# A mixture-of-experts loop: tokens gathered in four pieces and turned by VectorE, the down product copied by ScalarE alone

## The chip, the core and the metric

The kernel runs on one core of a Trainium2 chip. The metric is the device time of one execution in microseconds (us); the median of three runs before the change is 2490.03 us (2484.62 to 2492.65).

## What is computed

One decoder layer for 2048 tokens of width 1024: a mixer (windowed attention beside a gated recurrence), layer norm, and a mixture of experts: one shared expert and 64 routed ones, 8 for each token. The part that this change is about, from the reference, cut:

```python
def _moe(h, w_router, e_bias, w_gate, w_up, w_down, ws_gate, ws_up, ws_down):
    ...
    # pairs (token, expert) sorted by expert, padded to blocks of MOE_BLOCK = 128
    def body(acc, blk):
        toks, bw, e = blk
        xb = hp[toks]
        yb = (jax.nn.silu(xb @ w_gate[e]) * (xb @ w_up[e])) @ w_down[e]
        return acc.at[toks].add(yb.astype(f32) * bw[:, None]), None
```

All data is float32. Each product is made as three: every operand is split into a high part, rounded for TensorE (type `fp32r`), and the low rest, and high x high, high x low and low x high are summed.

## The kernel before

The program runs in phases: `mixer`, `output_and_route` (which leaves the table `htab`, one row of 1024 values and 64 expert weights for each token), `place_and_share` (which works out the token list of every block, `idx`, and half of the shared expert), `experts`, and `share_and_norm`. `experts` is a loop over blocks of 128 tokens, two blocks to a turn; an expert has as many blocks as its tokens fill. Its order is written out by hand: each engine has its own instruction stream (`block.tensor`, `block.vector`, `block.scalar`, `block.gpsimd`, `block.sync`) and they meet at semaphores.

For one block, in step n of the loop:

- GpSimd gathers the rows of block n+4 from `htab` into `xg` (128 tokens x 1088 values, `gather`, line 2301; its indices are first copied to `gi` by line 2298), copies the indices of block n to `si` (line 2319), and adds `y` to the rows of `acc` in DRAM by an indirect DMA (the scatter, line 2326). The scatter waits until the scatter before it has landed (`added`), since two blocks can hold one token.
- TensorE does the low part of gate and up for block n+1 (`gate_up_low`, line 2514, 8 matmuls), the down product of block n into `psY`, two halves of 512 columns (line 2559, 12 matmuls), the high part of gate and up for block n+2 (`gate_up_high`, line 2503, 16 matmuls), the turn of `H` (line 2521, 2 transposes into `psH`), and the turn of the tokens of block n+3 (`turn_x`, line 2487, 8 transposes of 128 x 128 into `psX`).
- ScalarE makes the high parts: `HT_hi`, `xT_hi` (line 2340, twice 512 columns out of `psX`), the silu into `sg`, the first half of `y` (line 2395), and, where a new expert begins, the high parts of the next expert's weights (line 2344: two pieces of gate and up, one of down).
- VectorE makes the low parts: `HT_lo` (line 2466), `xT_lo` (line 2406, twice), `pairw` (each token's weight for the expert, line 2434), `H` (line 2443), the second half of `y` (line 2476), and the low parts of the next weights (line 2409, three times 2048 columns for an expert).
- SyncE loads the raw weights of later experts (line 2284), two slots ahead, once `gulo_s` and `dlo_s` say that a slot's low parts are made.

`carry_wait` is a semaphore increment behind a wait; it costs an issue slot and nothing else.

## Time and profile before

| | us |
|---|---|
| median of three runs | 2490.03 |
| the profiled execution's own time | 2485.66 |
| its span in the profile | 2483.8 |
| `experts` loop, about | 853 to 2390 |
| TensorE busy | 2382.5 (96%) |
| VectorE busy | 1575.5 (63%) |
| ScalarE busy | 1161.9 (47%) |
| GpSimd busy | 767.3 (31%) |

A group of the profile gives a source line, the engine, the operation, destination and sources by the program's tile names, how often it ran, its busy time and mean duration, and the time that the engine was idle just before, with what ended most of that idle time. A timeline lists instructions by their start. Waits, semaphores and register instructions are not counted as busy. For DMAs, packets are counted by queue: queue 0 carries what GpSimd issues (gathers and scatters), queue 1 what SyncE issues (weights, in the loop); the share is of all 16 DMA engines' time.

### The profile page before, as it was taken

What the parts mean: (1) busy time and instruction counts of PE and PEld (TensorE: products, weight loads), DVE (VectorE), ACT (ScalarE), POOL (GpSimd) and SP (SyncE); (2) the same over time, 40 slices, a digit from 0 to 9 for tenths busy, and PEclk for the clock granted to TensorE, in tenths of its full rate; (3) what the DMA queues carried; (4) which work ended last, traced back from release to release, by engine and by line L of the source; (5) the groups of instructions that cost most, each with busy time, mean ns of one, the idle gap of its engine ahead of it and who ended that gap; (6) DMA issues with size and microseconds to landing.
All of it is one profiled execution on the core that took longest, in us unless ns stands there. A gap on an engine that the chain in (4) does not pass through costs nothing. (4 is left out here: it accounts for less than half of the span.)

```text
span 2483.8 us, 49979 instructions
## 1 busy us (share of the span) xinstructions
PE 2382.5 (96%) x11840; PEld 1954.7 (79%) x11842; DVE 1575.5 (63%) x2285; ACT 1161.9 (47%) x1621; POOL 767.3 (31%) x829
## 2 busy tenths in 40 slices
PE   8899999989997799999999999999999999999986
PEld 6677777678886688888888888888888888888875
DVE  6686867768878756555665555656665556655447
ACT  4525253542225645445554445545554445544334
POOL 0010100011110134334543433534443334444327
PEclk9999999989998899999999999999999999999998
DMA  7242323364445579778988878888888789987863
GB/s 254 77 144 98 111 94 111 117 218 164 171 164 206 196 230 284 223 219 270 273 259 233 254 218 263 268 266 262 257 253 243 224 223 274 283 247 222 216 221 136
DMA packets 253808, 524.34 MB, mean 211 GB/s; under 512 B 18065, under 2 KB 165169, under 8 KB 249649
## 3 DMA queue, kind: packets, MB, share of 16 engines
q1 hardware_dynamic: 204464, 336.64, 39.7%
q0 software_dynamic: 48672, 186.86, 29.4%
q8 instruction: 36, 0.59, 0.1%
q14 instruction: 28, 0.22, 0.0%
q10 hardware_dynamic: 608, 0.02, 0.0%
HBM read 386.61 MB, written 136.87 MB: 211 GB/s over the span
## 5 line engine op out<-in xcount | busy, mean ns | idle before, releaser
L2503 PE MATMUL psG<-gu_split,xT_hi 128*128 x2624 | 624.3, 390 | 2.9 <-ACT xT_hi L2340 1.5
L2503 PEld LDWEIGHTS psG<-gu_split,xT_hi 128*128 128x128 f32 x2624 | 493.8, 188 | 106.2 <-issue 3.6
L2326 POOL DMA_INDIRECT acc<-y,si x162 | 290.1, 1791 | 728.6 <-DMA acc<-y,si 413.3
L2409 DVE TENSOR_TENSOR gu_split<-raw_gu,gu_split (+1 forms) x127 | 290.6, 2288 | 175.3 <-ACT gu_split L2344 171.7
L2514 PE MATMUL psG<-gu_split,xT_lo 128*128 x1304 | 339.3, 402 | 5.9 <-issue 5.8
L2514 PEld LDWEIGHTS psG<-gu_split,xT_lo 128*128 128x128 f32 x1304 | 233.1, 188 | 50.1 <-issue 8.7
L2344 ACT ACTIVATE gu_split<-raw_gu x126 | 234.3, 1907 | 33.5 <-issue 33.5
L2301 POOL DMA_INDIRECT xg<-htab,gi x164 | 205.0, 1250 | 130.4 <-POOL gi L2298 109.7
L2409 DVE TENSOR_TENSOR d_lo<-raw_d,d_hi (+1 forms) x64 | 146.7, 2292 | 149.5 <-ACT d_hi L2344 149.5
L2389 ACT ACTIVATE HT_hi<-psH 128x256 fp32r<-128x256 f32 x162 | 62.4, 385 | 351.6 <-PE psH L2521 351.6
L2406 DVE TENSOR_TENSOR xT_lo<-psX,xT_hi 128x512 fp32r<-128x512 f32 x328 | 209.7, 680 | 8.5 <-ACT xT_hi L2340 8.5
L2476 DVE COPY y<-psY 128x512 f32<-128x512 f32 x162 | 111.4, 688 | 154.0 <-PE psY L2559 154.0
L2559 PE MATMUL psY<-d_hi,HT_hi 128*128 x648 | 199.9, 390 | 0.0
L2559 PE MATMUL psY<-d_lo,HT_hi 128*128 x648 | 199.7, 389 | 0.0
L2559 PE MATMUL psY<-d_hi,HT_lo 128*128 x648 | 199.6, 389 | 0.0
L2340 ACT ACTIVATE xT_hi<-psX 128x512 fp32r<-128x512 f32 x328 | 178.5, 596 | 17.6 <-PE psX L2487 9.2
L2487 PE MATMUL psX<-ident,xg 128*128 128x128 f32 x1320 | 171.7, 273 | 4.2 <-PEq L1639 4.2
L2376 ACT ACTIVATE sg<-psG 128x256 f32<-128x256 f32 x163 | 62.6, 384 | 204.3 <-PE psG L2514 204.3
L2344 ACT ACTIVATE d_hi<-raw_d (+1 forms) x64 | 122.7, 1917 | 74.6 <-PE psY L2559 74.5
L2487 PEld LDWEIGHTS psX<-ident,xg 128*128 128x128 f32 x1320 | 149.3, 141 | 4.7 <-issue 4.6
L2466 DVE TENSOR_TENSOR HT_lo<-psH,HT_hi 128x256 fp32r<-128x256 f32 x162 | 67.8, 418 | 131.0 <-ACT HT_hi L2389 130.5
L2395 ACT ACTIVATE y<-psY 128x512 f32<-128x512 f32 x162 | 95.6, 590 | 102.5 <-PE psY L2559 98.4
(388 smaller groups left out, 3723.7 us busy)
## 6 DMA issues: line engine op xcount, KB each, us to landing
raw_gu<-in_w_gate_dram SPq DMA_DIRECT2D x64, 1024.0 KB, 6.0
raw_gu<-in_w_up_dram SPq DMA_DIRECT2D x64, 1024.0 KB
raw_d<-in_w_down_dram SPq DMA_DIRECT2D x64, 1024.0 KB, 6.9
wring<-split_d SPq DMA_DIRECT2D x24, 1024.0 KB, 4.8
split_d<-wring POOLq DMA_DIRECT2D x8, 1024.0 KB, 4.2
raw_d<-mixed SPq DMA_DIRECT2D x16, 512.0 KB, 3.9
xt<-in_x_dram SPq DMA_DIRECT2D x16, 512.0 KB, 4.3
htab<-h SPq DMA_DIRECT2D x16, 512.0 KB, 2.6
```

The costliest lines, as they stand in the source:

```text
L2301: nc.gpsimd.indirect_dma_start(out=xg[slot][:], out_offset=None, in_=htab, in_offset=bass.IndirectOffsetOnAxis(ap=gi[slot][:, 0:1], axis=0 ...
L2326: nc.gpsimd.indirect_dma_start(out=acc, out_offset=bass.IndirectOffsetOnAxis(ap=si[k][:, 0:1], axis=0), in_=y[k][:], in_offset=None, compu ...
L2340: nc.scalar.activation(xT_hi[slot][:, h * HALF:(h + 1) * HALF, :], psX[h][:], ACT.Copy).then_inc(xhi_s[h], 1)
L2344: nc.scalar.activation(dst, src, ACT.Copy).then_inc(done, 1)
L2395: nc.scalar.activation(y[k][:, 0:512], psY[:, 0, :], ACT.Copy).then_inc(y_s[0], 1)
L2406: nc.vector.tensor_tensor(xT_lo[slot][:, at, :], psX[h][:], xT_hi[slot][:, at, :], ALU.subtract).then_inc(xlo_s[h], 1)
L2409: nc.vector.tensor_tensor(dst, src, hi, ALU.subtract).then_inc(dlo_s if n == 2 else gulo_s, 1)
L2476: nc.vector.tensor_copy(y[k][:, 512:], psY[:, 1, :]).then_inc(y_s[1], 1)
L2487: m = nc.tensor.transpose(psX[half][:, c, :], xg[slot][:, (half * HALF + c) * P:(half * HALF + c + 1) * P], ident[:])
L2503: nc.tensor.matmul(psG[slot][:], xT_hi[slot][:, c, :], right[:, bass.ds(w, 1), c, :].rearrange("p a n -> p (a n)"), start=(n == 0 and c == ...
L2514: m = nc.tensor.matmul(psG[slot][:], xT_lo[slot][:, c, :], gu_hi[:, bass.ds(w, 1), c, :].rearrange("p a n -> p (a n)"), start=False, stop= ...
L2559: m = nc.tensor.matmul(psY[:, h, :], left[:, c, :], right[:, bass.ds(w, 1), c, h * 512:(h + 1) * 512].rearrange("p a n -> p (a n)"), start ...
```

## The change

The table `htab` now has each row in four pieces (`QUADS`): 256 values and the weights of 16 experts, 272 values in all (`PIECE`). A gather is four indirect DMAs (`gather_pieces`, new line 1636), each with 128 indices. The indices are made ahead for all blocks (`pidx`), so that the piece g of partition group a holds quarter a of the tokens 32g to 32g+31. VectorE's transpose, which turns squares of 32 x 32, then gives the complete turn of the block: `xF`. To fit, value d of a token lies at chunk d mod 8 of partition d div 8, and the gate and up weights are loaded by rows in the same order (`by_run`, "(p k) n -> p k n"). The weights of the pairs are turned with them and turned back by one TensorE transpose into `psW`, from where `pairw` is read. `xT_hi` and `xT_lo` are made out of `xF` in SBUF, each by one instruction of 1024 columns. The whole of `y` is one ScalarE copy, and ScalarE also writes `gi` and `si`.

The core of the diff:

```diff
+def gather_pieces(nc, htab, to, at, done):
+    for g in range(QUADS):
+        nc.gpsimd.indirect_dma_start(out=to[:, g, 0:PIECE], out_offset=None, in_=htab.rearrange("r a w -> (r a) w"),
+                                     in_offset=bass.IndirectOffsetOnAxis(ap=at[:, g:g + 1], axis=0)).then_inc(done, 16)
...
@@ place_and_share, GpSimd @@
-            pool.wait_ge(idx_s, 2)
             for k in range(2):
-                nc.gpsimd.tensor_copy(gi[k][:], idx[:, k:k + 1]).then_inc(gi_s, 1)
+                nc.gpsimd.memset(xg[k][:, :, PIECE:WIDE], 0.0).then_inc(tails_s, 1)
+            pool.wait_ge(idx_s, 3)
...
@@ place_and_share, VectorE @@
+                for a in range(QUADS):
+                    for g in range(QUADS):
+                        last = nc.vector.tensor_scalar(pidx[a * QP:(a + 1) * QP, :, g], idx[g * QP:(g + 1) * QP, :], float(QUADS), float(a),
+                                                       ALU.mult, ALU.add)
...
@@ experts, GpSimd, in the loop @@
-                    pool.wait_ge(turned[1], s.n + 3)
-                    pool.wait_ge(pairw_s, s.n + 3)
+                    pool.wait_ge(next_gi_s, s.n + 1)
                     carry_wait(pool, passed)
-                    gather(s.n + AHEAD, k, s.n + AHEAD + 1)
-                    nc.gpsimd.tensor_copy(si[k][:], idx[:, bass.ds(s.n, 1)]).then_inc(si_s, 1)
+                    gather_pieces(nc, htab, xg[k], gi[k], x_in[k])
                     s.wait(pool, si_s)
-                    for h in range(2):
-                        s.wait(pool, y_s[h])
+                    s.wait(pool, y_s)
...
@@ experts, ScalarE @@
+            def high_x(nth, slot):
+                act.wait_ge(turned_s, nth)
+                nc.scalar.activation(xT_hi[slot][:], xF[slot][:, 0:KC, :], ACT.Copy).then_inc(xhi_s, 1)
...
-                    evac_x(s.n + 3, k)
+                    high_x(s.n + 3, k)
+                    gather_index(s.n + AHEAD, k)
...
-                    s.wait(act, yps_s[0])
-                    act.wait_ge(added[k], s.turn * 16)
-                    nc.scalar.activation(y[k][:, 0:512], psY[:, 0, :], ACT.Copy).then_inc(y_s[0], 1)
+                    s.wait(act, yps_s[1])
+                    scatter_index(s, k)
+                    nc.scalar.activation(y[k][:], psY[:].rearrange("p a b -> p (a b)"), ACT.Copy).then_inc(y_s, 1)
...
@@ experts, VectorE @@
+            def turn_x(slot, gathered, ahead):
+                dve.wait_ge(x_in[slot], gathered * 16 * QUADS)
+                if ahead is not None:
+                    dve.wait_ge(wturn_s, ahead)
+                    dve.wait_ge(xhi_s, ahead)
+                nc.vector.transpose(xF[slot][:, 0:KC, :].rearrange("p c (g j) -> p c g j", g=QUADS),
+                                    xg[slot][:, :, 0:D // QUADS].rearrange("p g (i c) -> p c g i", c=KC))
+                nc.vector.transpose(xF[slot][:, KC, :].rearrange("p (g j) -> p g j", g=QUADS),
+                                    xg[slot][:, :, D // QUADS:WIDE]).then_inc(turned_s, 1)
...
-                    for h in range(2):
-                        evac_x(h, s.n + 3, k)
                     s.wait(dve, H_s)
-                    pair_weight(nexts[n + 1], k, s.turn + 2)
+                    pair_weight(nexts[n], s.n + 2, 1 - k)
+                    low_x(s.n + 3, k)
                     product(s.n + 2, 1 - k)
+                    turn_x(1 - k, s.turn + k + 2, s.n + 2)
                     when_first(dve, nexts[n + 1], lambda: split(nexts[n + 1], 0))
-                    s.wait(dve, yps_s[1])
-                    dve.wait_ge(added[k], s.turn * 16)
-                    nc.vector.tensor_copy(y[k][:, 512:], psY[:, 1, :]).then_inc(y_s[1], 1)
                     when_first(dve, nexts[n + 1], lambda: split(nexts[n + 1], 1))
...
@@ experts, TensorE, at the end of a step @@
-                    pe.wait_ge(x_in[1 - k], (s.turn + k + 2) * 16 )
-                    for h in range(2):
-                        pe.wait_ge(xlo_s[h], s.n + 3)
-                        turn_x(1 - k, h)
+                    turn_weights(s.n + 3, k)
...
@@ weight loads, gate and up alone @@
-                        sp.dma_start(dst, w[0, bass.ds(e, 1)].rearrange("a (k p) n -> p (a k) n", p=P)).then_inc(sm, 16)
+                        rows = "a (k p) n -> p (a k) n" if sm is down_in else "a (p k) n -> p (a k) n"
+                        sp.dma_start(dst, w[0, bass.ds(e, 1)].rearrange(rows, p=P)).then_inc(sm, 16)
```

The stores and loads of `htab` rows in the phases before the loop follow the new layout; the 64 weights of a token go out as four runs of 16, one DMA for a tile of tokens where one for two tiles stood.

What stands on VectorE from `HT_lo` to the first weight split of a step, before (names as in the list above; ISA and REGISTER_ALU rows are waits and address arithmetic):

```order
L2466 TENSOR_TENSOR HT_lo<-psH,HT_hi 128x256
L2404 REGISTER_ALU
L2406 TENSOR_TENSOR xT_lo<-psX_0,xT_hi 128x512
L2406 TENSOR_TENSOR xT_lo<-psX_1,xT_hi 128x512
L2432 ISA
L2434 REGISTER_ALU
L2434 ISA
L2434 COPY pairw<-xg 128x1
L2438 REGISTER_ALU
L2443 SCALAR_TENSOR_TENSOR H_1<-psG_1,pairw,sg 128x256
```

And after the change:

```order
L2505 TENSOR_TENSOR HT_lo<-psH,HT_hi 128x256
L2468 REGISTER_ALU
L2470 REGISTER_ALU x2
L2470 ISA
L2470 COPY pairw<-psW 128x1
L2441 REGISTER_ALU
L2442 TENSOR_TENSOR xT_lo<-xF,xT_hi 128x1024
L2479 SCALAR_TENSOR_TENSOR H_1<-psG_1,pairw,sg 128x256
L2430 ISA
L2435 STREAM_TRANSPOSE xF<-xg 128x1024
L2437 STREAM_TRANSPOSE xF<-xg 128x128
```

The two `xT_lo` out of PSUM have become one out of `xF`, behind `pairw` now, and the turn of the next block's tokens (`STREAM_TRANSPOSE`, two instructions) follows `H`.

On GpSimd one block of the loop, before, from the index copy `gi` of the gather to the scatter:

```order
L2298 COPY gi<-idx 128x1
L2299 REGISTER_ALU
L2301 DMA xg<-htab,gi 128x1088
L2319 ISA
L2319 COPY si<-idx 128x1
L1099 REGISTER_ALU
L2324 REGISTER_ALU
L2326 DMA acc<-y_0,si 2176x1024
```

And after the change:

```order
L2335 ISA
L1636 DMA xg<-htab,gi 128x272 x4
L2340 REGISTER_ALU
L2342 DMA acc<-y_0,si 2176x1024
```

Both index copies have left GpSimd, and four DMAs of 128 x 272 stand where one of 128 x 1088 stood.

On VectorE just ahead of the loop, in `place_and_share`, where the block lists `idx` become ready, before and after:

```order
L1945 TENSOR_SCALAR some<-psRank 128x192
L1946 TENSOR_TENSOR idx<-none,some 128x192
L1947 TENSOR_SCALAR idx<-zr,blockno 128x4
L2030 TENSOR_TENSOR gu_split<-raw_gu,gu_split 128x2048
```

```order
L1958 TENSOR_SCALAR some<-psRank 128x192
L1959 TENSOR_TENSOR idx<-none,some 128x192
L1960 TENSOR_SCALAR idx<-zr,blockno 128x4
L1965 TENSOR_SCALAR pidx<-idx 32x196 x16
L2049 TENSOR_TENSOR gu_split<-raw_gu,gu_split 128x2048
```

Sixteen instructions for `pidx` stand between `idx` and the split of the first expert's weights.

## Rows read from the trace of the kernel before

**Rows 1.** The page: its span.

```profile
span 2483.8 us, 49979 instructions
```

**Rows 2.** Windows: us, busy of each engine, clock, DMA share, GB/s.

```profile
1500.00:2000.00 500.00, 496.82 (x2455) 416.43 (x2454) 291.43 (x384) 251.57 (x331) 206.31 (x216) 1.00 0.86 252
```

**Rows 3.** Timeline of TensorE, one block: start us, us, line, operation, count.

```profile
1513.30 0.38 PE L2521 MATMUL psH<-ident,H 128*128 128x128 f32 x2
1513.52 1.04 PE L2487 MATMUL psX<-ident,xg 128*128 128x128 f32 x8
1514.31 2.09 PE L2514 MATMUL psG<-gu_split,xT_lo 128*128 x8
...
1518.95 3.79 PE L2503 MATMUL psG<-gu_split,xT_hi 128*128 x16
1522.59 0.38 PE L2521 MATMUL psH<-ident,H 128*128 128x128 f32 x2
```

**Rows 4.** Tile psH over the loop: ns min/median/max, first and last start.

```profile
L2521 PE MATMUL psH<-ident,H x322: 270/271/272, 880.1 to 2373.8; 128*128 128x128 f32 x161
```

**Rows 5.** Groups on VectorE in the loop: busy us, mean ns, idle before.

```profile
L2409 DVE TENSOR_TENSOR gu_split<-raw_gu,gu_split x124 | 283.7, 2288 | 171.7 <-ACT gu_split L2344 171.7
L2406 DVE TENSOR_TENSOR xT_lo<-psX,xT_hi 128x512 fp32r<-128x512 f32 x322 | 205.9, 680 | 8.3 <-ACT xT_hi L2340 8.3
L2409 DVE TENSOR_TENSOR d_lo<-raw_d,d_hi x62 | 142.1, 2292 | 148.9 <-ACT d_hi L2344 148.9
L2476 DVE COPY y<-psY 128x512 f32<-128x512 f32 x161 | 110.7, 688 | 152.0 <-PE psY L2559 152.0
L2443 DVE SCALAR_TENSOR_TENSOR H<-psG,pairw,sg 128x256 f32<-128x256 f32 x161 | 77.1, 479 | 32.0 <-ACT sg L2376 31.9
L2466 DVE TENSOR_TENSOR HT_lo<-psH,HT_hi 128x256 fp32r<-128x256 f32 x161 | 67.3, 418 | 130.5 <-ACT HT_hi L2389 130.5
```

**Rows 6.** A group on ScalarE in the loop, same columns.

```profile
L2340 ACT ACTIVATE xT_hi<-psX 128x512 fp32r<-128x512 f32 x322 | 175.1, 596 | 8.3
```

**Rows 7.** The scatter on GpSimd in the loop, same columns.

```profile
L2326 POOL DMA_INDIRECT acc<-y,si x161 | 288.5, 1792 | 726.3 <-DMA acc<-y,si 413.3 <-DVE pairw L2434 146.3 <-DVE y L2476 56.8
```

**Rows 8.** Gather and scatter on GpSimd: ns min/median/max, first and last start.

```profile
L2301 POOL DMA_INDIRECT xg<-htab,gi x161: 1004/1007/3114, 884.1 to 2377.7; - x161
L2326 POOL DMA_INDIRECT acc<-y,si x162: 1583/1607/2717, 878.4 to 2381.2; - x162
```

**Rows 9.** Timeline of VectorE and GpSimd, start and us: a wait for the port.

```profile
1300.11 2.28 DVE L2409 TENSOR_TENSOR gu_split<-raw_gu,gu_split  x1
...
1301.18 2.69 POOL L2326 DMA_INDIRECT acc<-y,si  x1 [3.99 <-DVE y L2476]
```

**Rows 10.** DMA queues, 1200 to 1600 us: packets, MB, share of 16 engines.

```profile
q0 software_dynamic: 12121, 45.52, 45.0%
q1 hardware_dynamic: 41648, 55.17, 41.3%
```

**Rows 11.** Line 2326, the scatter: time to landing.

```profile
DMA to landing us min/median/max: 6.0/7.5/11.4
```

**Rows 12.** DMA queue 0, 2382 to 2389 us: one scatter alone.

```profile
q0 software_dynamic: 144, 0.52, 48.8%
```

**Rows 13.** DMA queue 0, 2372.5 to 2382 us: one scatter, one gather.

```profile
q0 software_dynamic: 288, 1.08, 53.7%
```

**Rows 14.** Timeline of SyncE: issues of gate weights for three experts.

```profile
1330.62 0.38 SPq L2284 DMA_DIRECT2D raw_gu<-in_w_gate_dram  x1
...
1358.48 0.38 SPq L2284 DMA_DIRECT2D raw_gu<-in_w_gate_dram  x1
...
1377.05 0.38 SPq L2284 DMA_DIRECT2D raw_gu<-in_w_gate_dram  x1
```

**Rows 15.** Timeline of VectorE before the loop starts.

```profile
839.59 0.36 DVE L1945 TENSOR_SCALAR some<-psRank 128x192 f32<-128x192 f32 x1
...
852.94 2.29 DVE L2409 TENSOR_TENSOR gu_split<-raw_gu,gu_split 128x2048 fp32r<-128x2048 f32 x1 [3.06 <-PEq L1639]
```

More of the change, by code:

```diff
@@ L2128, in _, with load_expert, experts @@
                     down(n)
-def load_expert(eng, w_gate, w_up, w_down, expert, slot, wgu, wd, loaded):
+def load_expert(eng, w_gate, w_up, w_down, expert, slot, wgu, wd, loaded, by_run=False):
     for w, sm, dst in zip((w_gate, w_up, w_down), loaded, (wgu[:, slot, :, 0:FE], wgu[:, slot, :, FE:], wd[:, slot])):
-        eng.dma_start(dst, w[0, expert].rearrange("(k p) n -> p k n", p=P)).then_inc(sm, 16)
-def experts(nc, passed, w_gate, w_up, w_down, ident, htab, acc, table, n_turns, idx, xg, gi, gi_s, x_in, acc_out, gu, guhi_s, gulo_s, wgu, wd, loaded, y, si, added,
+        rows = "(p k) n -> p k n" if by_run and w is not w_down else "(k p) n -> p k n"
+        eng.dma_start(dst, w[0, expert].rearrange(rows, p=P)).then_inc(sm, 16)
+def experts(nc, passed, w_gate, w_up, w_down, ident, htab, acc, table, n_turns, idx, pidx, tails_s, xg, gi, gi_s, x_in, acc_out, gu, guhi_s, gulo_s, wgu, wd, loaded, y, si, added,
             prefetch_shared, prefetch_hT):
@@ L2166, in experts @@
         psG = [ps(f"psG5_{i}", [P, 2 * FE]) for i in range(2)]
-        psX = [ps(f"psX5_{i}", [P, HALF, P]) for i in range(2)]
+        psW = ps("psW5", [P, P])
         psH = ps("psH5", [P, 512])
@@ L2203, in __init__, with column @@
                 self.word = word
-            def expert(self):
-                return within(self.word & (EXPERTS - 1), 0, EXPERTS - 1)
+            def column(self):
+                share = EXPERTS // QUADS
+                return within((self.word & (EXPERTS - 1)) + (self.word & (EXPERTS - share)), 0, P - 1)
             def next(self):
@@ L2483, in _, with turn_weights @@
         def _(pe):
-            def turn_x(slot, half):
-                for c in range(HALF):
-                    m = nc.tensor.transpose(psX[half][:, c, :], xg[slot][:, (half * HALF + c) * P:(half * HALF + c + 1) * P], ident[:])
-                m.then_inc(turned[half], 1)
+            def turn_weights(nth, slot):
+                pe.wait_ge(turned_s, nth)
+                if not (isinstance(nth, int) and nth == 1):
+                    pe.wait_ge(pairw_s, nth - 1)
+                carry_wait(pe, passed)
+                nc.tensor.transpose(psW[:], xF[slot][:, KC, :], ident[:]).then_inc(wturn_s, 1)
             def gate_up_high(nth, slot, entry):
-                for h in range(2):
-                    pe.wait_ge(xhi_s[h], nth)
+                pe.wait_ge(xhi_s, nth)
                 pe.wait_ge(gulo_s, entry.rank() * 2)
@@ L2535, in _ @@
             turn_H(0)
-            pe.wait_ge(x_in[0], 32)
-            for h in range(2):
-                pe.wait_ge(xlo_s[h], 2)
-                turn_x(0, h)
+            turn_weights(2, 1)
             def body(i):
@@ L2545, in body @@
                     gate_up_low(s.n + 2, 1 - k, words[n + 1])
-                    for h in range(2):
-                        s.wait(pe, y_s[h], behind=1)
+                    s.wait(pe, y_s, behind=1)
                     pe.wait_ge(dlo_s, r)
@@ L3122, in decoder_layer @@
         si = [sb(f"si{i}", [P, 1], I32) for i in range(2)]
-        experts(nc, passed, w_gate, w_up, w_down, ident, htab, acc, table, n_turns, idx, xg, gi, gi_s, x_in, acc_out, gu, guhi_s, gulo_s, raw_gu, raw_d,
+        experts(nc, passed, w_gate, w_up, w_down, ident, htab, acc, table, n_turns, idx, pidx, tails_s, xg, gi, gi_s, x_in, acc_out, gu, guhi_s, gulo_s, raw_gu, raw_d,
                 loaded, y, si, added,
```

134 lines of the change are left out of this document (71 added, 63 removed).

## Prediction

> **What bounds the kernel now.** I read the page first, for the span [rows 1], then the windows, then single steps. In the window from 1500 to 2000 us TensorE is busy 496.8 of 500 us at granted clock 1.00, and the DMA engines 0.86 of their time [rows 2]. So the loop is bound by TensorE with DMA close behind. The 161 turns of `H` from 880.1 to 2373.8 us give a period of 1493.7 / 160 = 9.336 us a block [rows 4]; an undisturbed step has 9.29 (1513.30 to 1522.59) [rows 3]. VectorE, ScalarE and GpSimd have idle time, but their groups must be read by step, since each has waits of its own.
>
> **TensorE.** The eight transposes of tokens take 0.79 us (1513.52 to 1514.31) [rows 3]. One transpose of the same shape stays, for the weights. Gain: 7/8 x 0.79 = 0.69 us a step, all of it on the path, since nothing waits ahead of them. The floor of a step is then 9.29 - 0.69 = 8.60 us. `psX` is no longer a wait for TensorE; what comes late next is one of the following.
>
> **VectorE, a step.** Removed: two `xT_lo` of 0.68 and the half of `y`, 0.69, together 2.05 us [rows 5]. Added: one `xT_lo` of 1024 columns and two turns. From 512 columns in 0.68 and 2048 in 2.29 us the slope is 1.05 ns a column, so 1024 columns take 1.22 us. No row shows a VectorE transpose. Its nearest row is the same 1.22 for 1024 columns; the small turn of 128 columns lies between 0 and the 0.42 of 256 columns, I take 0.3. Above, each element might cost more, because the source is read with a step of 8 values; twice the slope gives 2.3 us. Weight splits stay: 62 experts x 3 x 2.29 / 161 = 2.65 us a step. Sum with `HT_lo` 0.42, `H` 0.48 and 0.15 for `pairw`: 0.42 + 0.48 + 0.15 + 1.22 + 1.22 + 0.3 + 2.65 = 6.4 us, at double price 7.5. Both are under 8.60, so the cost is covered by TensorE's work. In a step with splits it isn't quite: the down split waits for ScalarE's high part, which now starts behind a whole `y`, and `HT_lo` of the next block is queued behind it, with TensorE waiting in the middle of the down product. I charge 0.05 us a step for that, bounds 0 and 0.2.
>
> **ScalarE.** `xT_hi` was 2 x 0.60 [rows 6] and becomes one instruction; `y` grows from one half to two, about 0.5 us more, and two index copies are new, some 0.2 each. It had 47% of its time busy (table), so this is nothing by itself.
>
> **GpSimd.** A gather issue takes 1.01 us and a scatter 1.61 [rows 8]. I price the issue by its 128 indices, since a scatter of nearly the same bytes costs more: four pieces 4 x 1.01 = 4.04, with the scatter 5.65 us a step, where 2.62 stood. Removed are two index copies. The upper end comes from a wait: the scatter that began at 1301.18, while `gu_split` (1300.11 to 1302.39) was running, took 2.69 in place of 1.61 us [rows 9]; the longest gather has 3.1 [rows 8]. `gu_split`, `d_lo` and the new `xT_lo` are all of that kind, two sources in SBUF: 2.65 + 1.22 = 3.87 us a step, and with `y` gone from between the two `gu_split` these stand back to back. If all of that were lost, GpSimd would need 5.65 + 3.87 = 9.5 us. If half is, 7.6. I take half, as an issue already under way isn't stretched and only a start inside is.
>
> The Trainium skill has this rule (SBUF — State Buffer, "Who interferes with whom"): a VectorE instruction with two SBUF inputs excludes a GpSimd instruction that reads SBUF, whoever is first keeps the shared interface to its end, and one with a single SBUF input doesn't. By that rule, the trace agrees (2.69 against 1.61), and the new turns, with one source, would add nothing to the 3.87.
>
> **DMA.** In 400 us (43 blocks) queue 0 has 45.0% and queue 1 41.3% of 16 engines [rows 10]: per block 0.450 x 400 / 43 = 4.2 us of all engines for gather and scatter. 55.17 MB at 3.146 MB an expert are 17.5 experts, so the weights of one take 0.413 x 400 / 17.5 = 9.4 us. Weight issues stand 27.9 and 18.6 us apart [rows 14]: experts have three or two blocks, 62 of them over 161 blocks means 37 and 25. An expert of three needs 9.4 + 12.6 = 22.0 us against 3 x 8.60 = 25.8; one of two needs 17.8 against 17.2. That is no longer covered.
>
> The pieces add to this. A scatter alone has 0.488 x 7 x 16 = 54.7 engine-us [rows 12], scatter and gather 0.537 x 9.5 x 16 = 81.6 [rows 13], so a gather of 128 rows has 26.9. As 512 pieces of 1088 bytes at the 63 ns of queue 1's mean packet of 1325 bytes (0.413 x 6400 us / 41648) it has 32.5. That is 0.35 us of all engines a block; lower end 0 (same bytes). The experts of two blocks then need up to 18.5 us. Between 17.2 and 18.5 I take 18.2, 9.1 a step, near the upper end because the prefetch reaches only two slots. For three blocks I take 8.65.
>
> The scatter also makes a chain: each waits for the landing of the one before, 6.0 to 11.4 us, median 7.5 [rows 11], and 77 of these waits took 413 us of GpSimd's time [rows 7]. The median fits in 8.60, the long ones with weights in the queue don't; 18.2 includes that.
>
> **Start.** Sixteen `pidx` instructions of 196 elements at 0.36 us (192 elements) [rows 15] are 5.8 us on VectorE just ahead of the loop, which starts at 852.94 after VectorE, GpSimd and SyncE are all through. The eight gather pieces queue behind them, and the first weight split moves behind a turn (1.5 us). Together +7 us, bounds 4 and 11. The `htab` stores and loads are in pieces of 1 KB and 64 bytes, with 8 more DMA issues at 0.38 us; they lie beside mixer and routing work of TensorE. If that cover were gone they would cost 3 us. `by_run` changes which rows a partition gets, the pieces stay 1 KB: nothing, or a gain of contiguous reads that I don't count.
>
> **Sum.** Loop period: (50 x 9.1 + 111 x 8.65) / 161 = 8.79, plus VectorE's 0.05, less what overlaps: 8.8. 162 blocks x (9.336 - 8.8) = -86.8 us; start +7. The profiled execution has 2485.66 us, span 2483.8 [rows 1] and 1.9 around it. 2485.7 - 86.8 + 7 = 2405.9, about 2406. It lies 4 us under the median of the runs (2490.03), inside their spread.
>
> **Rivals.** *TensorE alone decides (0.20).* The queues have slack enough, by their averages: DMA 0.86 x 9.336 + 0.35 = 8.4 us a step, under 8.60. Against it stand the experts of two blocks. -0.736 x 162 + 7 = -112: 2373; with seven transposes at 0.11 about 2362.
>
> *The queue takes the gain back (0.13).* Each piece waits its own turn behind weight packets in the rings; `x_in` comes late, VectorE stands in `turn_x` with the weight splits behind it. A period of 9.2 gives 2485.7 - 22 + 7 = 2471; at 9.29 nothing is left.
>
> *GpSimd becomes the bound, slower (0.14).* Five indirect DMAs a block, each start able to meet a VectorE instruction that holds the port. From 9.29 us on (9.336 - 7/162) the kernel is slower, that is when port and landing waits cost over 3.64 us beside the 5.65. The 3.87 of two-source time does it: 9.5 gives 2485.7 + 27 + 7 = 2519; with the turns' 1.5 counted too, 11.0 gives 2762. For it speak rows 9, against it that an issue under way isn't stretched.
>
> *The turn by VectorE is dear, slower (0.08).* It decides when the large turn costs over 1.22 + (9.29 - 6.4) = 4.1 us. At four times the row's 1.22 the step is 10.1, 2485.7 + 124 + 7 = 2617. The source is read with a step of 32 bytes; the trace of before has no such read to judge by. The Trainium skill (SBUF — State Buffer, "Door 1") says that lines are 16 bytes and every access that comes to a new line pays, so strides are free up to 4 fp32 values; no row here shows it, and it names no factor.
>
> That the change doesn't do what it says is excluded by the order of the instructions.
>
> **How the numbers follow.** Forecast 0.45, at 2380 to 2440. A measurement of this kernel can tell about 0.3%, 7.5 us. Faster: 0.45 + 0.20 + two thirds of the queue's case, 0.73; within 0.3%: 0.06, the rest of it and a little of GpSimd's; slower 0.21. The range reaches from 2358 (TensorE alone, with a little more) to 2500 (the queue's case and the near end of GpSimd's), which leaves out some 0.2.
>
> **What would show it.** Right: period 8.7 to 8.9, TensorE with idle time of about 0.2 us a step before `psG` or `psY`, concentrated on experts of two blocks; DMA share 0.93 or more in the window from 1500 to 2000; gather pieces of 1.0 us each. `STREAM_TRANSPOSE` at 1.2 to 1.4 us. Wrong: pieces that cost much more or less than 1.0; a turn over 2.5; TensorE without idle time (first rival); GpSimd busy over 90% of the step.

## The result, and the profile after

The changed kernel takes 2588.92 us (median of 4 runs, 2579.47 to 2594.74) where the kernel before takes 2487.32 (4 runs beside it): 1.040 times as long, 95% interval 1.036 to 1.044. Forecast were 2406 us and a range of 2358 to 2500. The profiled execution has a span of 2584.0 us.

Span, and the window from 1500 to 2000 us (us, then busy time of PE, PEld, DVE, ACT, POOL, then granted clock, DMA share, GB/s), against [rows 1, 2]:

```profile
span 2584.0 us, 47703 instructions
...
1500.00:2000.00 500.00, 457.31 (x1975) 367.55 (x1976) 357.72 (x367) 260.52 (x368) 357.69 (x252) 0.96 0.85 239
```

TensorE has gone from 496.8 to 457.3 of 500 us, GpSimd from 206.3 to 357.7. The DMA share is nearly what it was, 0.85 for 0.86. The granted clock is 0.96 where it was 1.00: after some of TensorE's waits it stands at 1.2 GHz for 3.4 or 6.8 us. That makes a matmul of `gate_up_high` 398 ns in the mean in place of 389, some 0.3 us a step by all matmuls, and TensorE is idle for 0.8 us a step beside it, so the clock isn't the bound.

TensorE's timeline for one undisturbed block, against [rows 3], and tile `psH` over the loop, against [rows 4]:

```profile
1508.27 0.38 PE L2558 MATMUL psH<-ident,H 128*128 128x128 f32 x2
1508.49 0.27 PE L2527 MATMUL psW<-ident,xF 128*128 128x128 f32 x1
1508.52 2.09 PE L2551 MATMUL psG<-gu_split,xT_lo 128*128 x8
...
1513.17 3.79 PE L2541 MATMUL psG<-gu_split,xT_hi 128*128 x16
1516.80 0.38 PE L2558 MATMUL psH<-ident,H 128*128 128x128 f32 x2
```

```profile
L2414 ACT ACTIVATE HT_hi<-psH x162: 372/387/389, 887.0 to 2474.7; 128x256 fp32r<-128x256 f32 x162
```

The same row of the kernel before:

```profile
L2389 ACT ACTIVATE HT_hi<-psH x162: 385/385/388, 870.1 to 2374.1; 128x256 fp32r<-128x256 f32 x162
```

An undisturbed step has 8.53 us (1508.27 to 1516.80). But the period is 9.86: `HT_hi`, once a step, begins first at 887.0 and the 162nd time at 2474.7, and 1587.7 / 161 = 9.86. Before, by the same row, it was 9.34. The 161 periods cost 84 us more, the first `HT_hi` begins 17 us later, and what follows the last one takes as long as before (109 us for 110). Together that is the 100 us between the two spans.

The groups of the whole program (busy us, mean ns, idle before them and its releasers), against [rows 5, 7]:

```profile
L1636 POOL DMA_INDIRECT xg<-htab,gi x664 | 829.6, 1249 | 238.9 <-issue 190.9 <-ACT gi L2360 40.2 <-ACT y L2421 6.4
L2435 DVE STREAM_TRANSPOSE xF<-xg 128x1024 f32<-128x1024 f32 x165 | 352.9, 2139 | 267.3 <-DMA xg<-htab,gi 259.8 <-issue 7.2
L2342 POOL DMA_INDIRECT acc<-y,si x162 | 301.2, 1859 | 251.1 <-DMA acc<-y,si 191.0 <-issue 36.7 <-ACT y L2421 13.5
L2442 DVE TENSOR_TENSOR xT_lo<-xF,xT_hi 128x1024 fp32r<-128x1024 f32 x164 | 199.9, 1219 | 17.8 <-ACT xT_hi L2355 10.6 <-issue 7.0
```

Divide GpSimd's two rows by 162 blocks: pieces 5.1, idle ahead of them 1.5, scatter 1.9, idle ahead of it 1.55, together 10 us a block (the pieces gathered ahead of the loop are counted in, so it is a little over the period): its own work and one large foreign wait, the landing of the last scatter (191 us, 1.2 a block). For ScalarE's index or `y` it waits only some 60 us in the whole program. Its stream is full; every other engine has slack.

GpSimd's timeline shows why the parts of that stream add up. Start and us; the last row is VectorE's, from its own timeline:

```profile
1549.76 1.62 POOL L2342 DMA_INDIRECT acc<-y,si  x1 [3.13 <-DMA acc<-y,si]
1551.69 0.99 POOL L1636 DMA_INDIRECT xg<-htab,gi  x1 [0.31 <-issue]
...
1559.15 1.62 POOL L2342 DMA_INDIRECT acc<-y,si  x1 [2.72 <-DMA acc<-y,si]
1561.08 0.99 POOL L1636 DMA_INDIRECT xg<-htab,gi  x1 [0.30 <-issue]
1562.38 0.95 POOL L1636 DMA_INDIRECT xg<-htab,gi  x1 [0.30 <-issue]
1563.63 3.05 POOL L1636 DMA_INDIRECT xg<-htab,gi  x1 [0.30 <-issue]
1566.99 1.89 POOL L1636 DMA_INDIRECT xg<-htab,gi  x1 [0.31 <-issue]
1569.19 1.91 POOL L2342 DMA_INDIRECT acc<-y,si  x1 [0.30 <-issue]
...
1563.57 4.49 DVE L2445 TENSOR_TENSOR gu_split<-raw_gu,gu_split  x2 [0.39 <-issue]
```

"Port" stands here for what [rows 9] showed: a GpSimd instruction that meets a VectorE instruction with two sources in SBUF takes longer. From 1549.76 to 1559.15 the scatter waits for the landing of the one before: a step of 9.39 us set by a chain of DMA. From 1559.15 to 1569.19 a pair of `gu_split` stretches two pieces by 2.1 and 0.9 us: a step of 10.04 set by the port. Counted from scatter to scatter over all 161 steps, three kinds of step stand beside each other. The 55 steps in which VectorE begins two `gu_split` take 10.4 us in the mean; their four pieces take 6.6 in place of 3.8, and only one of these steps waits for a landing. The 57 steps with `d_lo` alone take 10.5, and 49 of them wait for a landing. The other 49 take 8.5, what TensorE needs. So both causes are at work, each in its own steps, and the remaining steps lose nothing in the mean.

The start, in VectorE's and GpSimd's timelines:

```profile
845.36 5.57 DVE L1965 TENSOR_SCALAR pidx<-idx 32x196 int32<-32x196 int32 x16
...
867.34 2.00 DVE L2435 STREAM_TRANSPOSE xF<-xg 128x1024 f32<-128x1024 f32 x1 [7.02 <-issue]
...
851.00 2.30 POOL L1810 COPY gi<-pidx 128x4 int32<-128x4 int32 x1 [81.82 <-DVE pidx L1965]
853.60 1.12 POOL L1636 DMA_INDIRECT xg<-htab,gi  x1 [0.29 <-POOL gi L1810]
```

`pidx` takes 5.57 us, the index copy behind it 2.30 (a `gu_split` began at 850.97), and eight pieces follow at 1.26. The loop begins at 867.34 where it began at 852.94, 14 us later; 3 us more are lost between there and the first `HT_hi`.

### The profile page after: what moved, and what is told of

Its sections match the earlier page's. It is cut to its first block and busy times, and to the rows that moved or that the text cites. A ratio compares the mean times of both kernels' runs of the same rounds, so it can differ in the third digit from the quotient of the medians.

```text
span 2584.0 us, 47703 instructions
## 1 busy us (share of the span) xinstructions
PE 2344.0 (91%) x10684; PEld 1865.7 (72%) x10686; DVE 1835.5 (71%) x2304; ACT 1229.0 (48%) x1781; POOL 1270.5 (49%) x1005
## 5 line engine op out<-in xcount | busy, mean ns | idle before, releaser
L1636 POOL DMA_INDIRECT xg<-htab,gi x664 | 829.6, 1249 | 238.9 <-issue 190.9
L2435 DVE STREAM_TRANSPOSE xF<-xg 128x1024 f32<-128x1024 f32 x165 | 352.9, 2139 | 267.3 <-DMA xg<-htab,gi 259.8
L2587 PE MATMUL psY<-d_hi,HT_lo 128*128 x648 | 223.7, 429 | 111.1 <-DVE HT_lo L2505 88.9
L2587 PEld LDWEIGHTS psY<-d_hi,HT_lo 128*128 128x128 f32 x648 | 124.9, 203 | 162.2 <-issue 139.8
L2355 ACT ACTIVATE xT_hi<-xF 128x1024 fp32r<-128x1024 f32 x164 | 172.8, 1053 | 110.7 <-DVE xF L2437 110.7
L2442 DVE TENSOR_TENSOR xT_lo<-xF,xT_hi 128x1024 fp32r<-128x1024 f32 x164 | 199.9, 1219 | 17.8 <-ACT xT_hi L2355 10.6
L2365 ACT ACTIVATE si<-idx 128x1 int32 x162 | 31.9, 197 | 345.8 <-PE psY L2587 301.2
L2421 ACT ACTIVATE y<-psY 128x1024 f32<-128x1024 f32 x162 | 163.5, 1009 | 0.0
L2587 PEld LDWEIGHTS psY<-d_hi,HT_hi 128*128 128x128 f32 x648 | 126.0, 195 | 33.0 <-issue 5.8
L2587 PEld LDWEIGHTS psY<-d_lo,HT_hi 128*128 128x128 f32 x648 | 127.4, 197 | 28.2
```

Of the source, the lines that this page charges most:

```text
L1636: nc.gpsimd.indirect_dma_start(out=to[:, g, 0:PIECE], out_offset=None, in_=htab.rearrange("r a w -> (r a) w"), in_offset=bass.IndirectOffs ...
L2355: nc.scalar.activation(xT_hi[slot][:], xF[slot][:, 0:KC, :], ACT.Copy).then_inc(xhi_s, 1)
L2421: nc.scalar.activation(y[k][:], psY[:].rearrange("p a b -> p (a b)"), ACT.Copy).then_inc(y_s, 1)
L2435: nc.vector.transpose(xF[slot][:, 0:KC, :].rearrange("p c (g j) -> p c g j", g=QUADS), xg[slot][:, :, 0:D // QUADS].rearrange("p g (i c) - ...
L2442: nc.vector.tensor_tensor(xT_lo[slot][:], xF[slot][:, 0:KC, :], xT_hi[slot][:], ALU.subtract).then_inc(xlo_s, 1)
L2587: m = nc.tensor.matmul(psY[:, h, :], left[:, c, :], right[:, bass.ds(w, 1), c, h * 512:(h + 1) * 512].rearrange("p a n -> p (a n)"), start ...
```

## Experiments

Three theories. **G**: GpSimd's stream (issues, port waits, landing waits) took TensorE's place. **V**: VectorE's turn, 2.14 us, in VectorE's strict order of instructions, took it. **L**: the smaller packets land late behind the weights. Later **B** came, a burst of indirect DMAs that delays a signal, for a cost that none of these has. Each run's time stands beside runs of the kernel before on the same chip (2489.6 to 2490.5).

### Which engine: one gather, a cheaper turn, no landing wait

**One gather of whole rows in the changed kernel** (the core of the edit; the counts that are waited for and the index tile follow it).

```diff
-    for g in range(QUADS):
-        nc.gpsimd.indirect_dma_start(out=to[:, g, 0:PIECE], out_offset=None, in_=htab.rearrange("r a w -> (r a) w"),
-                                     in_offset=bass.IndirectOffsetOnAxis(ap=at[:, g:g + 1], axis=0)).then_inc(done, 16)
+    nc.gpsimd.indirect_dma_start(out=to[:].rearrange("p a w -> p (a w)")[:, 0:QUADS * PIECE], out_offset=None, in_=htab.rearrange("r a w -> r (a w)"),
+                                 in_offset=bass.IndirectOffsetOnAxis(ap=at[:, 0:1], axis=0)).then_inc(done, 16)
```

> The changed kernel with one gather DMA of 128 whole rows a block in place of the four pieces; everything behind it stays, so what VectorE turns is not the whole turned block (the tokens of a group stay in their own 32 partitions and the products are of wrongly arranged features): only the time is meant. It takes 3 x 1.26 = 3.8 us of issue a block from GpSimd. Theory G (GpSimd's time a step, five issues of 6.9 us with gaps and landing waits, is the bound that took the place of TensorE): the period falls from 9.86 to 8.6 to 8.9 us, the time to 2385 to 2430. Theory V (VectorE's turn of 2.14 us in its in-order stream is the bound): the period stays within 0.2 us of 9.86, the time over 2550. Theory L (landing of gathered rows behind weights in the queues): as V at first, since the same bytes land, with a gain of at most half, 2480 to 2550.

2453.69 us, 0.984 times before (0.982 to 0.986), 135 us under the changed kernel. V, with over 2550, is far off; L, with 2480 at least, is missed by 26 us and G, with 2430 at most, by 24. The rows say where G's 24 us are (loop from 900 to 2400 us, then the DMA issues: number and median us to landing):

```profile
L2342 POOL DMA_INDIRECT acc<-y,si x161 | 291.4, 1810 | 947.5 <-DMA acc<-y,si 860.3 <-issue 38.4 <-ACT gi L2360 28.6
L1635 POOL DMA_INDIRECT xg<-htab,gi x161 | 161.3, 1002 | 54.1 <-issue 47.8 <-ACT gi L2360 6.0 <-ACT y L2421 0.3
...
acc<-y,si POOLq DMA_INDIRECT x161, 8.6
```

GpSimd now waits 860 us for landings. The median landing is 8.6 us where it was 7.5 [rows 11], but that is no growth: landings fall in two groups, about 6 to 8 and 8.5 to 11 us, and the mean over the 162 scatters is 8.15 here and was 8.20 before. In both kernels a scatter that waited for a landing starts 0.80 us after it. So a chain in which every scatter waits for the one before takes 8.15 + 0.80 = 8.95 us a step, and the period is 9.03.

**The turn reads with step 1.** `"p g (i c) -> p c g i"` becomes `"p g (c i) -> p c g i"` in `turn_x`.

> The changed kernel, but the large turn reads its source with a step of 1 value in place of 8; the features then stand in another order than the rows of the weights, so the products are of wrongly paired features: only the time is meant. It tells whether the 2.14 us of the turn come from the step, and what they are worth. If the step is the cause the turn takes 1.1 to 1.3 us, else 2.1. Theory V: every microsecond of it is on the path, 0.9 x 162 = 150 us less, 2440. Theory G: VectorE only waits more ahead of the turn; the turn's result comes 0.9 us sooner for the index of the next gather, which helps a little: 2560 to 2590. Theory L: no change.

2568.52 us (1.032, 1.029 to 1.035).

```profile
L2435 DVE STREAM_TRANSPOSE xF<-xg 128x1024 f32<-128x1024 f32 x154 | 191.2, 1241 | 284.5 <-DMA xg<-htab,gi 282.9 <-issue 1.4
```

The step is the price: 1.24 us with step 1, 2.14 with step 8. It is worth 20 us of the 100, and VectorE's wait for rows ahead of it grew from 250 to 283 (from 900 to 2400 us). V had asked for 2440, G for 2560 to 2590. Another way to read the turn is thus no cure.

**Odd blocks are added to a second table**, so that a scatter waits for the one two blocks back.

```diff
-                    pool.wait_ge(added[1 - k], (s.turn + k) * 16)
+                    pool.wait_ge(added[k], s.turn * 16)
...
-                    nc.gpsimd.indirect_dma_start(out=acc, out_offset=bass.IndirectOffsetOnAxis(ap=si[k][:, 0:1], axis=0),
+                    nc.gpsimd.indirect_dma_start(out=acc[k], out_offset=bass.IndirectOffsetOnAxis(ap=si[k][:, 0:1], axis=0),
```

> The changed kernel, but the blocks of odd number are added to a second table in DRAM that nothing reads, so their share is left out of the output. Each scatter then waits for the landing of the one two blocks back instead of the last one; nothing else is removed. The changed kernel's GpSimd waits 191 us (70 times) for a landing. If this chain is what lifts GpSimd over TensorE's 8.6 us (theory G with the landing as its decisive part), the period falls by up to 191 / 162 = 1.2 us, to 8.7 to 9.1 and the time to 2400 to 2460. If GpSimd's issues alone are the bound, the wait only moves to another place and the gain is under 40 us, 2550 to 2585. Theory V: no change.

2481.67 us (0.9945, 0.993 to 0.996): 107 us gained, of the 191 us that GpSimd waited for landings. That is under G's 129 to 189 us: the period of the profiled execution, the slowest of the five (2498.98), is 9.33, 0.8 over TensorE's step. What keeps it there is found below.

**Both edits together.**

> The changed kernel with one gather of whole rows in place of four pieces (what VectorE turns is then wrongly arranged) and with the blocks of odd number added to a second table that nothing reads (their share is left out of the output): both edits of the earlier two runs together. Alone they gave 2453.69 and 2481.67 us. With one gather GpSimd waited 860 us for landings, 5.3 us a step, and its period was 9.03. If the landing of the scatter is what held that kernel above TensorE's 8.53, the period now falls to 8.6 to 8.7, the time to 2380 to 2400. Theory V: VectorE's 2.4 us of turns a step keep it at 8.9 to 9.0, 2440 to 2450.

2396.49 us (0.962, 0.961 to 0.964). The window from 1500 to 2000 us:

```profile
1500.00:2000.00 500.00, 498.46 (x2242) 402.82 (x2241) 402.19 (x416) 293.16 (x416) 179.22 (x115) 1.00 0.90 271
```

TensorE is busy 498.5 of 500 us at clock 1.00. VectorE with its dear turn, ScalarE with all of `y` and the queues all fit under it. V is out: what the changed kernel lacks is time on GpSimd and the landing.

### Pieces, order and y, one at a time

**The kernel before with its gather in four pieces** of 272 columns.

```diff
-                nc.gpsimd.indirect_dma_start(out=xg[slot][:], out_offset=None, in_=htab,
-                                             in_offset=bass.IndirectOffsetOnAxis(ap=gi[slot][:, 0:1], axis=0)).then_inc(x_in[slot], 16)
+                for a in range(4):
+                    nc.gpsimd.indirect_dma_start(out=xg[slot][:, a * 272:(a + 1) * 272], out_offset=None, in_=htab,
+                                                 in_offset=bass.IndirectOffsetOnAxis(ap=gi[slot][:, 0:1], axis=0),
+                                                 element_offset=a * 272).then_inc(x_in[slot], 16)
```

> The kernel before, with its gather in four DMAs of a quarter of each row (272 values) and nothing else changed. It adds 3 x 1.26 = 3.8 us of issue a block to GpSimd; TensorE's work and its 9.3 us a step stay. Theory G (GpSimd's stream of issues and its wait for the scatter's landing are the bound of the changed kernel): the same stream of four pieces at 1.26, a scatter at 1.85 and 1.2 to 1.6 us of waits stands here too, so the period goes to 9.7 to 9.9 us, the time to 2550 to 2580. Theory V (VectorE's turn and order): nothing, 2485 to 2495. Theory L (small packets land late): something between, with VectorE or TensorE waiting for the rows, 2500 to 2540.

2672.01 us (1.073, 1.071 to 1.074), 92 us over the upper end of G's range. From 900 to 2400 us:

```profile
L2304 POOL DMA_INDIRECT xg<-htab,gi x574 | 780.6, 1360 | 247.8 <-issue 134.7 <-POOL gi L2300 113.1
L2330 POOL DMA_INDIRECT acc<-y,si x143 | 234.2, 1638 | 139.0 <-POOL si L2323 67.3 <-issue 40.6 <-DMA acc<-y,si 21.2
L2300 POOL COPY gi<-idx 128x1 int32 x143 | 146.7, 1026 | 3.0 <-DVE pairw L2438 3.0
```

I had forgotten that here GpSimd copies its own indices, 1.0 us in the mean with a gap of 0.8 behind it. These rows and the copy of `si` (32 us) fill the window, the step is 10.44 us, and of GpSimd's idle time only 24 us are waits for anything but its own stream (21 for a landing). So the pieces alone, with no turn by VectorE, do the harm. That giving the index copies to ScalarE is a help follows from these rows; no run tried it alone.

**The turn behind the splits.**

> The changed kernel with the turn moved behind the weight splits in VectorE's order, so that no split stands behind a wait for gathered rows. Theory G: GpSimd's stream stays as it is; the turn comes later only in steps with splits, whose index for the next gather comes up to 4.6 us later, and this may cost: 2575 to 2630. Theory V (the order of VectorE holds the splits and TensorE): waits of TensorE for HT_lo (111 us) and half of VectorE's 256 us of waits for rows go, 2480 to 2520.

2698.55 us (1.083, 1.081 to 1.085).

```profile
POOL xg L1636 <- ACT gi L2360: 249.7, 122, 2.8
```

GpSimd, which waited 29 us for its index in the changed kernel (from 900 to 2400 us), now waits 250 us in 122 waits: turn, index, pieces, their landing, turn is a ring, and a turn that comes up to 4.6 us late is paid by the next gather. The turn in front is the better of the two places. Both theories' numbers were wrong here.

**The second half of `y` back on VectorE.**

> The changed kernel with the second half of y copied by VectorE again, as in the kernel before. Theory G: GpSimd is the bound and y is seldom what it waits for (under 10 us in all), so 2575 to 2600. If the whole copy by ScalarE is worth something here, this kernel is slower by up to 0.7 us a step of VectorE's time, 2600 to 2700. If the later y costs, it is faster, 2540 to 2575.

2630.90 us (1.058, 1.053 to 1.063), 42 us over the changed kernel. From 900 to 2400 us pieces take 1306 ns in the mean in place of 1269, and TensorE waits 104 us for VectorE's half. The whole copy by ScalarE is worth having.

**The kernel before with the whole of `y` by ScalarE.**

> The kernel before with the other half of the change alone: the whole of y leaves PSUM by one ScalarE copy, none by VectorE. It takes 0.69 us a step from VectorE and one wait from GpSimd; the scatter may start some 0.3 us later. All theories: TensorE stays the bound at 9.3 us, 2480 to 2495, no measurable change. If the later y cost something by itself, as in a later scatter that keeps the next gather back, this kernel would be slower by 0.3 us a step or more, 2535.

2483.33 us, 0.9978 (0.9964 to 0.9991) in 10 runs against 13. TensorE is busy 499.97 of 500 us. As expected, nearly nothing: 0.2%, less than the runs differ among themselves. Still, no other kernel here with all of its output right is below the kernel before.

### The port, and a cost that nobody had asked for

**VectorE's low parts with one source in SBUF.** A tile `psZ` of zeros in PSUM takes the place of the high part.

```diff
-                nc.vector.tensor_tensor(dst, src, hi, ALU.subtract).then_inc(dlo_s if n == 2 else gulo_s, 1)
+                zero = bcast(psZ[:].rearrange("p a b -> p (a b)"), 1, 2) if n == 2 else bcast(psZ[:, 0, :], 1, 4)
+                nc.vector.tensor_tensor(dst, src, zero, ALU.subtract).then_inc(dlo_s if n == 2 else gulo_s, 1)
```

> The changed kernel, but VectorE's three kinds of low part (both gate and up splits, the down split, xT_lo) subtract zeros that lie in PSUM in place of the high part in SBUF. So the low parts are not low parts and the products are wrong: only the time is meant. Same instructions, same sizes, one source in SBUF in place of two. If the two-source instructions are what stretches the pieces from 0.95 to 1.25 us and the scatter from 1.61 to 1.86, both go back, 4 x 0.30 + 0.25 = 1.45 us a step less for GpSimd; the landing wait then takes part of it, as with one gather (9.03): period 9.0 to 9.3, 2450 to 2500. If the pieces stay at 1.25, the stretch is something else and the time stays at 2575 to 2600.

2535.51 us (1.018, 1.015 to 1.021).

```profile
L1636 POOL DMA_INDIRECT xg<-htab,gi x628 | 601.6, 958 | 525.2 <-ACT gi L2362 370.6 <-issue 150.1 <-ACT y L2423 2.4
L2344 POOL DMA_INDIRECT acc<-y,si x157 | 255.4, 1627 | 116.4 <-issue 67.1 <-ACT y L2423 42.6 <-DMA acc<-y,si 6.7
```

The port part is exact: pieces 0.96, scatter 1.63, VectorE's instructions as long as before (2.27, 1.22). By the Trainium skill (SBUF — State Buffer, "Who interferes with whom") a VectorE instruction with two SBUF inputs contends with a GpSimd instruction that reads SBUF, and one with at most one SBUF input doesn't; the two kernels agree (pieces of 1.25 us with two, 0.96 with one). The time isn't as forecast: it lies 36 us over the range, and GpSimd stands idle for want of an index. The next experiment takes the landing wait away as well.

> The run with one source in SBUF for VectorE's low parts, with the blocks of odd number added to a second table that nothing reads as well (both parts of the output wrong as told for those runs). All four pieces stay. GpSimd's stream is then 4 x (0.95 + 0.30) + 1.61 + some 0.5 of waits = 7.1 us a step and its wait for the last landing is gone: TensorE's 8.53 should decide, period 8.55 to 8.8, 2385 to 2430. If pieces that land late behind weights matter by themselves (theory L), it stays over 8.9, 2440.

2540.69 us (1.020, 1.017 to 1.022), no gain at all, where both alone give 53 and 107. Timelines of TensorE, ScalarE and GpSimd in the run with one source:

```profile
1510.61 0.38 PE L2563 MATMUL psH<-ident,H 128*128 128x128 f32 x2
1519.51 0.38 PE L2563 MATMUL psH<-ident,H 128*128 128x128 f32 x2
...
1512.35 0.39 ACT L2416 ACTIVATE HT_hi<-psH 128x256 fp32r<-128x256 f32 x1 [3.82 <-PE psH L2563]
1521.80 0.38 ACT L2416 ACTIVATE HT_hi<-psH 128x256 fp32r<-128x256 f32 x1 [3.14 <-remote]
...
1510.26 1.63 POOL L2344 DMA_INDIRECT acc<-y,si  x1 [0.30 <-issue]
1519.62 1.63 POOL L2344 DMA_INDIRECT acc<-y,si  x1 [0.31 <-issue]
```

The transposes of `H` end at 1510.99 and 1519.89, TensorE has gone on to its next matmuls (from 1510.86 and 1519.76), ScalarE is free, and `HT_hi` begins at 1512.35 and 1521.80: 1.4 and 1.9 us late, each half a microsecond after a scatter's end. The trace also has the increment of the semaphore that `HT_hi` waits for, at 1512.33 and 1521.78. So it is the signal that is late, not ScalarE. A start more than 0.3 us after both the transposes and ScalarE's last instruction is found in 136 of the loop's 162 steps here, in 78 with the second table, in 30 in the changed kernel, and in none in the kernel before or with one gather. `HT_hi` feeds the down product, and the index of the next pieces stands behind it on ScalarE, so the delay goes into the ring of turn, index and pieces.

**B, a pause.** B says that the delays come when five indirect DMAs run with no gap but 0.30 us. Between the fourth piece and the scatter:

```diff
+                    nc.gpsimd.memset(idle[:], 0.0).then_inc(idle_s, 1)
+                    s.wait(pool, idle_s)
                     s.wait(pool, si_s)
```

> The run with one source in SBUF for VectorE's low parts (same parts of the output wrong), with one memset of 128x1024 and a wait for it put on GpSimd between the fourth piece and the scatter, about 1.4 us a step. In that run HT_hi began 0.9 to 2.2 us after the last transposes of H in 133 of 155 steps, with ScalarE free, and always within some 0.5 us of the end of a scatter that had followed four pieces without a gap; in the kernel before and with one gather it begins 0.04 us after. Theory B (the late signal comes with a burst of five indirect DMAs without a gap): the pause breaks the burst, most of the delays go and with them up to 1.3 us a step, 2400 to 2460, though GpSimd does more. Theory G alone (GpSimd's stream decides, whatever is in it): 1.4 us more a step, of which 2.5 us of waits for the index can take all: 2535 to 2600.

2506.91 us (1.006, 1.004 to 1.008). `HT_hi` is late in 6 of 162 steps in place of 136, and the kernel is 29 us faster although GpSimd does more. The time lies between the two forecasts: memset and wait take 1.87 us a step, and from 900 to 2400 us GpSimd waits 198 us for landings again (7 in the run without the pause). With a memset of one column the pause is 1.0 us (0.12, and 0.90 of wait):

> All three costs of GpSimd's stream taken away with the four pieces left in: one source in SBUF for VectorE's low parts (port), the second table for odd blocks (landing wait; both parts of the output wrong as told before), and a memset of 128x1 with a wait, about 1.0 us, between the fourth piece and the scatter (burst). GpSimd's stream is 4 x 1.25 + 1.0 + 1.93 = 7.9 us a step, under TensorE's 8.53. If port, landing and burst are all that the changed kernel loses, TensorE decides alone: period 8.55 to 8.65, 2390 to 2415. If the pieces cost something more (late rows in the queue, a fourth thing), 2440 or more.

2397.86 us (0.963, 0.961 to 0.965), with all four pieces.

```profile
1500.00:2000.00 500.00, 498.98 (x2247) 404.04 (x2246) 402.89 (x419) 295.53 (x416) 321.31 (x346) 1.00 0.96 271
```

TensorE 499.0 of 500, period (2288.3 - 890.1) / 161 = 8.68, just over the forecast 8.65. Port, landing and burst are the whole loss in the loop: with the three gone the kernel is within 2 us of the one with a single gather and a second table. Nothing is left for the pieces' packets, so L is out, at a DMA share of 0.96. Against the run with one source and the second table (2540.69) this one differs by the pause alone, and it is worth 143 us.

Two rivals of B can be looked up in the traces, counting the signals at which ScalarE was free. One says that a signal is late whenever it falls into a scatter, burst or not, and that the pause only moves the scatter away from it. It doesn't hold: here 131 signals fall into a scatter and none is late, with one gather and the second table 84 and none; with one source and no pause all 92 signals that fall into a scatter 0.3 us behind the fourth piece are late, by 1.6 us in the mean. The other says that any idle gap as long as the pause would do. It doesn't hold either: in the two runs with one source and no pause the scatter sometimes comes late by itself, and after an idle gap of 0.9 to 1.2 us 8 of 15 signals are still late (after more than 1.6 us none of 9). So something in the memset or in the wait for it helps beyond the time that they take. What, isn't known.

> The run with the second table for odd blocks (their share left out), with the same short pause of about 1.0 us between the fourth piece and the scatter. There HT_hi began over 0.3 us after the last transposes of H in 79 of 161 steps. Theory B: most of these delays go, some 0.6 us a step, but the pause adds 1.0 to a stream that was 8.5 us, so the time comes out within 20 us of the 2481.67 of that run. Theory G alone: the pause is all in the stream, 0.5 to 1.0 us a step more, 2560 to 2640.

2453.68 us (0.988, 0.984 to 0.993): 28 us less than without the pause, more than B's 20, and no late `HT_hi` is left. The pause costs nothing there, it gains.

> The changed kernel, all of its output right, with the same short pause alone. Its HT_hi was late in only 27 of 151 steps, some 30 us in all; its GpSimd waits 1.2 us a step for the last scatter's landing, and the pause can lie in that wait. Expected from the two together: between 20 us less and 60 us more, 2565 to 2650. Clearly under 2565 would say that the burst costs the changed kernel more than the late signals counted.

2585.49 us (1.039, 1.037 to 1.041), no different from the changed kernel, though no `HT_hi` is late any more. There GpSimd is full in either case.

**The turn once more, beside the second table.** With VectorE's turn on step 1 as well as the second table:

> The changed kernel with the second table for odd blocks (their share left out) and the turn reading with step 1 (features in another order than the weights). Alone they gave 2481.67 and 2568.52 us (-107 and -20). If VectorE's turn matters only through GpSimd, 0.9 us less of it gives about 20 us again or nothing: 2455 to 2485. If VectorE becomes the bound once the landing wait is gone (theory V), 0.5 to 0.8 us a step is gained, TensorE near alone: 2390 to 2430.

2480.90 us (0.996, 0.994 to 0.997) against 2481.67: the turn's 0.9 us is worth nothing there, and V is out a second time. A correct kernel with two tables would have to zero the second and add it at the end; a wait only at the first block of an expert would do without, since one expert's blocks hold different tokens. Neither was run.

## Why the prediction was wrong

- **TensorE: right.** Forecast floor 8.60, undisturbed step 8.53, and 8.68 as a period once nothing else is in the way. The time that TensorE alone gives is 2397, not 2362 to 2373: the start is dearer than the forecast by 8 to 13 us, and the period 0.1 over the floor.
- **GpSimd: the step that failed.** The prediction had GpSimd's step at 5.65 us plus half of 3.87 for the port, under 8.60, with the landing wait beside it. Measured is a stream of 9.86 us. The 5.65 was made of medians, "4 x 1.01", beside [rows 8]; missing were 0.30 us of gap before every piece and before most scatters (1.4 us a step), which the trace of before could not show with a single gather. The port term, half of 3.87, was too high if anything: 4 x 0.30 + 0.25 = 1.45 measured. Issues of 5.4, port 1.45 and gaps 1.4 give 8.3, still under 8.53.
- **The landing: the decisive omission.** I let the scatter's landing wait stand beside GpSimd's sum ("the median fits in 8.60"). It lies inside it: 1.2 us a step. With 0.3 of waits for `gi` and `y` the sum is 9.8 of the 9.86. The median was also the wrong number. The mean landing of before is 8.20 us, and the next scatter starts 0.80 after it, so the chain by itself takes 9.0 us a step, over 8.60 before anything was changed. I took the 413 us of [rows 7] for slack that would go when the step got shorter; it was a chain near its limit, and a shorter step meets it first.
- **Averages.** Steps with two `gu_split` are set by the port (10.4 us) and steps with `d_lo` by the landing (10.5), while the others run at 8.5. A sum by averages hides that two thirds of the steps belong to kinds that take over 10 us, each for a reason of its own.
- **The rival that came true** is "GpSimd becomes the bound", with 0.14, but by other terms than its own. Its condition was port and landing waits of over 3.64 us beside the 5.65. Measured are 1.45 + 1.2 = 2.65; the gaps between issues, which it doesn't name, bring the rest. That its price of 9.5 a step, 2519 us, is near the 9.86 is in part luck.
- **A term that nobody had:** the late signal. In the changed kernel it is small (30 of 162 steps, 27 us, nothing gained when it is cured alone); it decides as soon as port and landing are out of the way.
- **VectorE: wrong in size, right in effect.** The turn costs 2.14 us, not 1.22; the bound of 2.3 from twice the slope held. Its step of 8 is worth 20 us in the changed kernel and nothing beside the second table. The rule of the Trainium skill beside that rival (SBUF — State Buffer, "Door 1", an access that comes to a new 16-byte line pays) agrees in kind: a step of 32 bytes costs 1.7 times a step of 4.
- **ScalarE: nothing by itself, right**, and giving it all of `y` is worth 42 us in the changed kernel. What the index copies are worth there wasn't run.
- **DMA: the wrong bound.** Two-block experts were to need 18.2 us, 9.1 a step. The run with a DMA share of 0.96 goes at 8.68 a step over all experts.
- **Start:** +14 us at the loop's entry and +17 at the first `HT_hi`, for +7 with a bound of 11. The `pidx` term was right (5.57 for 5.8); the port wait of the first index copy (2.30 us where the second takes 0.20) and the pieces' 1.26 were not in it.

## What to carry to other kernels

Count an in-order engine's whole stream for one step as the new bound would see it: mean durations, the gap ahead of each instruction, and its waits for foreign work, which don't overlap with its own. A long wait of an engine is slack only if what it waits for gets faster with the step; the landing of this chain of scatters didn't (8.20 us in the mean before, 8.15 with one gather at a shorter step). Take a chain's mean and the time from landing to next start, not its median. When two removals gain less together than one alone, look for a delay that has no instruction of its own: the start of the consumer against the end of its producer.

## What the runs showed of the hardware

- An indirect DMA that gathers 128 rows costs GpSimd 0.98 to 1.01 us (median) with rows of 4352 bytes and 0.99 for the first, 0.95 for each further one with rows of 1088 bytes. 0.30 us lie between two in a row.
- A scatter with add of 128 rows of 4 KB lands after 8.2 us in the mean in the loop of the kernel before, in two groups (about 6 to 8 and 8.5 to 11 us). A scatter that waits for it starts 0.80 us later.
- VectorE's transpose of 128x1024 fp32 takes 1.24 us from a source read with step 1 and 2.14 with step 8; 128x128 takes 0.27.
- Around a burst of five indirect DMAs 0.30 us apart TensorE's semaphore increment comes late: by 1.3 us in the mean of all 162 steps with one source, by up to 2.2 there and 2.5 with the second table. A memset of one column and a wait for it, 1.0 us ahead of the fifth DMA, cures it (0 of 162 steps in each of three runs), where an idle gap of 0.9 to 1.2 us leaves 8 of 15 late. Through what the burst acts, and what the memset or its wait does, wasn't found. In the kernel before with four pieces, where index copies stand in between, the delay is hardly seen (3 of 162 steps).
